# Attention with the keys on the partitions, 512 queries at a time, in rounded parts, in a two-block network kernel

## The reference, cut to what matters

```python
def one_block(qblk):
    s = jnp.einsum('bqhgd,bkhd->bhgqk', qblk, k, preferred_element_type=jnp.float32) * scale
    p = jax.nn.softmax(s, axis=-1).astype(v.dtype)
    return jnp.einsum('bhgqk,bkhd->bqhgd', p, v)
...
y = jnp.concatenate([ya * jax.nn.silu(a_gate), yb * jax.nn.silu(b_gate)], axis=-1)
return y @ w_out
```

## Time and profile before

| | us |
|---|---|
| median of 3 runs | 4312.03 |
| lowest, highest | 4309.52, 4312.44 |
| the profiled execution | 4309.44 |
| its span in the profile | 4307.4 |
| attention: pooling products to the last unit | 360.0 to 670.5 |
| ev_out: first to last weight product | 672.0 to 821.2 |
| granted clock of TensorE, mean | 0.98 |

### The profile page before, as it was taken

One profiled execution on the slowest core, in us unless ns is written; L12 is line 12 of the kernel. 1 busy time (PEld: TensorE's weight loads), 2 busy tenths in 40 slices (PEclk: granted clock), 3 DMA queues, 4 the chain that ended last, 5 costly groups with the idle time before them and its releaser, 6 DMA issues.

```text
span 4307.4 us, 51362 instructions
## 1 busy us (share of the span) xinstructions
PE 4077.1 (95%) x20059; PEld 3120.8 (72%) x20059; DVE 2023.9 (47%) x2420; ACT 1270.5 (29%) x1883; POOL 1333.3 (31%) x791
## 2 busy tenths in 40 slices
PE   7999998899999998889999999999999899999998
PEld 5776775457777774578888788876766678878886
DVE  4263662864676776571443233324444654323322
ACT  3122330212222221231332232224554633223222
POOL 0530000011111111022344444434444544444443
PEclk8999999999999999999999999999999999999999
DMA  6111004331121115651233333321000033333333
GB/s 229 39 39 59 0 0 141 142 136 65 68 76 68 68 53 191 155 163 49 83 93 97 98 97 97 98 89 69 25 25 25 16 113 94 96 99 97 97 98 107
DMA packets 118829, 372.05 MB, mean 86 GB/s; under 512 B 18004, under 2 KB 33679, under 8 KB 114896
## 3 DMA queue, kind: packets, MB, share of 16 engines
q1 hardware_dynamic: 98960, 296.38, 22.1%
q0 software_dynamic: 12784, 59.50, 3.8%
q10 hardware_dynamic: 6928, 13.96, 0.9%
HBM read 329.37 MB, written 38.06 MB: 85 GB/s over the span
## 4 chain that ended last, share of the span: by engine, by line
PE 63%; issue 16%; DVE 8%; POOL 6%; DMA 3%; ACT 2%; SPq 0%; POOLq 0%; ACTq 0%; DVEq 0%
PE banks L276 22%; PE banks L3104 6%; POOL w_parts L261 6%; PE banks L1230 5%; PE banks L291 5%; PE banks L696 5%; PE banks L1605 4%; PE banks L982 3%; PE banks L3178 2%; PE banks L3207 2%; DVE neg_max L1061 2%; DMA w_ring<-in_weights 1%; PE banks L3194 1%; PE banks L1586 1%; PE banks L1636 1%
## 5 line engine op out<-in xcount | busy, mean ns | idle before, releaser
L261 POOL TENSOR_TENSOR w_parts<-w_ring,w_parts 128x1024 fp32r<-128x1024 f32 x344 | 843.1, 2452 | 1089.3 <-ACT w_parts L254 1087.2
L276 PE MATMUL banks<-x_high,w_parts 128*128 128x512 f32 x2944 | 912.1, 390 | 0.0
L254 ACT ACTIVATE w_parts<-w_ring 128x1024 fp32r<-128x1024 f32 x344 | 364.5, 1060 | 1281.7 <-PE banks L276 1273.8
L276 PEld LDWEIGHTS banks<-x_high,w_parts 128*128 128x128 f32 x2944 | 552.6, 188 | 116.8 <-issue 2.1
L276 PE MATMUL banks<-x_low,w_parts 128*128 128x512 f32 x1472 | 572.8, 389 | 0.0
L276 PE MATMUL banks<-hidden_high,w_parts 128*128 128x512 f32 x1600 | 482.2, 392 | 6.0 <-POOL w_parts L261 6.0
L3312 DVE TENSOR_TENSOR_SCAN arena<-arena,flags 128x128 f32<-128x128 f32 (+3 forms) x192 | 248.7, 1308 | 250.3 <-ACT arena L3253 248.5
L276 PEld LDWEIGHTS banks<-hidden_high,w_parts 128*128 128x128 f32 x1600 | 301.7, 189 | 71.0 <-POOL w_parts L261 6.8
L2993 DVE TENSOR_TENSOR hidden_high<-banks,gate_temps 128x512 f32 (+1 forms) x88 | 60.9, 692 | 571.7 <-PE banks L276 571.6
L276 PEld LDWEIGHTS banks<-x_low,w_parts 128*128 128x128 f32 x1472 | 276.3, 188 | 59.0 <-issue 1.9
L1230 PE MATMUL banks<-parts_b,w_ring_low 128*128 128x512 f32 x896 | 303.6, 405 | 14.7 <-DVE resid_low L394 9.7
(11 more groups left out here) (456 smaller groups left out, 6488.4 us busy)
## 6 DMA issues: line engine op xcount, KB each, us to landing
w_ring<-in_weights SPq DMA_DIRECT2D x488, 512.0 KB, 3.5
arena<-in_hy_dft SPq DMA_DIRECT2D x11, 1536.0 KB, 6.1
s_cl<-arena POOLq DMA_DIRECT2D x4, 1152.0 KB, 6.7
resid<-in_xT ACTq DMA_DIRECT2D x2, 2048.0 KB, 26.3
resid<-in_xT POOLq DMA_DIRECT2D x1, 4096.0 KB, 14.0
arena<-in_fn_seq POOLq DMA_DIRECT2D x1, 4096.0 KB, 18.0
resid_spill<-resid POOLq DMA_DIRECT2D x1, 4096.0 KB, 12.6
s_e<-arena POOLq DMA_DIRECT2D x4, 1024.0 KB, 5.1
```

Of the source, the lines that this page charges most:

```text
L254: nc.scalar.activation(WP[:, g % 2, 0, :], WR[:, (g % RING) * TILE:(g % RING + 1) * TILE], ACT.Identity).then_inc(w_hi, 1)
L261: nc.gpsimd.tensor_tensor(WP[:, g % 2, 1, :], WR[:, (g % RING) * TILE:(g % RING + 1) * TILE], WP[:, g % 2, 0, :].bitcast(F32), ALU.subtrac ...
L276: mm = nc.tensor.matmul(PS[:, bank + h // H, :], w[a][:, k % KB, :], srcs[b][:, k, at + h:at + h + H], start=(first and i + q == 0), stop= ...
```

## The change

One half is now 512 queries of one head (12 halves), and a block is 128 of the 1280 keys (120 blocks in all, index i; half g, block b in it). Keys are on the partitions, queries on the free axis, so nothing is transposed.

- Keys, queries and values are split in rounded parts: high by ScalarE (`keys_high`, `queries_high`, `values_high`), low by GpSimd (`keys_low`, `queries_low`, `values_low`), all in memory that `resid` and `arena` leave free.
- The maximum of a query is still needed. `tops` multiplies 128 queries by 1280 keys, high parts only, into banks 4 to 6; VectorE's `top` takes the maximum. Four of these are turned by one transpose (`turned`), VectorE's `shift` spreads them on four partitions, and a fourth product of each block, of four rows, subtracts them (`MINUS`, `SHIFT`).
- `scores`: three products of parts and that fourth one, into bank i % 4. ScalarE takes the exponential twice, once unrounded (`PROB`), once rounded (`PPARTS[0]`). GpSimd's `prob_low` is their difference. `values`: three products of parts into bank 7.
- VectorE's `summed` adds `PROB` over the ten blocks; `denominator` sums it over the partitions by a product with ones; `divided` takes the reciprocal of 512 columns and multiplies; `gated` multiplies by the gate before.
- Three buffers each for `PROB` and its parts: the exponential of block i waits for sum and low part of block i-3 and, for the rounded copy, for its value products.
- The load of x is issued when the last value products are done, in two halves, as the parts of keys and values lie there. TensorE begins ev_out's modulation tiles one VectorE step earlier.
- Loops are written out.

```diff
...
-    A_P, A_PT, A_QC = A_S0, A_S0 + 2 * KEYS, A_S0 + 4 * KEYS
...
+    SHIFT = [PTB_[:, 8192 + 3584:8192 + 4096], s0_parts(7040, H)]
+    PROB = [ar(A_S0 + 4 * H + i * H, H) for i in range(3)]
+    PPARTS = [[s0_parts(7 * H + i * H, H) for i in range(3)], [s0_parts(at_, H) for at_ in (5120, 5632, 6400)]]
+    VPARTS = [[t[:, at_ + kv * KEYS:at_ + (kv + 1) * KEYS].rearrange("p (b n) -> p b n", b=KEYS // P)
+               for kv in range(N_KV)] for t, at_ in ((PTB_, 8192), (XLOW_, 2 * N_KV * KEYS))]
+    ACCP = [ar(2560 + i * H, H) for i in range(2)]
+    MINUS = s0_parts(6912, P)
+    TOP = [ar(A_S0 + 7552 + 4 * i, 4) for i in range(2)]
...
+    KBL = KEYS // P
+    HALVES = 2 * N_HEADS
+    BLOCKS = KBL * HALVES
...
+            def tops(g, t):
+                p.wait_ge(a_hi, parts_made(g))
+                p.wait_ge(a_top, 4 * g + t)
+                if t == 0 and g >= 3:
+                    p.wait_ge(a_o, 2 * (g - 2))
                 for c in range(0, KEYS, H):
                     w = min(H, KEYS - c)
...
+                    mm = nc.tensor.matmul(PS[:, 4 + c // H, 0:w], QPARTS[g % 2][0][:, t * P:(t + 1) * P],
+                                          KPARTS[0][kv_of(g)][:, c:c + w], start=True, stop=True)
+                mm.then_inc(a_mx, 1)
+            def turned(g):
+                p.wait_ge(a_top, 4 * g + 4)
+                if g:
+                    p.wait_ge(a_sh, g)
+                nc.tensor.transpose(PS[0:4, 6, 384:512], TOP[g % 2], IDENT[:, :]).then_inc(a_tt, 1)
+            def scores(i):
+                g, b = divmod(i, KBL)
+                kv, q = kv_of(g), QPARTS[g % 2]
+                if b == 0:
+                    p.wait_ge(a_lo, parts_made(g))
+                if i == 2:
+                    p.wait_ge(pme, 4)
+                if i >= 4:
+                    p.wait_ge(a_p, i - 3)
+                out_ = PS[:, i % 4, :]
+                for n, (x, y) in enumerate(((0, 0), (0, 1), (1, 0))):
+                    nc.tensor.matmul(out_, KPARTS[x][kv][:, b * P:(b + 1) * P], q[y], start=(n == 0), stop=False)
+                if b == 0:
+                    p.wait_ge(a_sh, g + 1)
+                nc.tensor.matmul(out_, MINUS[0:4, :], SHIFT[g % 2][0:4, :], start=False, stop=True).then_inc(a_s, 1)
+            def values(i):
+                g, b = divmod(i, KBL)
+                p.wait_ge(a_pl, i + 1)
+                if b == 0:
+                    p.wait_ge(a_lo, 3 if g < HALVES // N_KV else 6)
+                    if g:
+                        p.wait_ge(a_o, 2 * g - 1)
+                for n, (x, y) in enumerate(((0, 0), (1, 0), (0, 1))):
+                    mm = nc.tensor.matmul(PS[:, 7, :], VPARTS[x][kv_of(g)][:, b, :], PPARTS[y][i % 3],
+                                          start=(b + n == 0), stop=(b == KBL - 1 and n == 2))
+                mm.then_inc(a_pv, 1)
+            def denominator(g):
+                p.wait_ge(a_ad, KBL * (g + 1))
+                p.wait_ge(a_top, 4 * min(g + 3, HALVES))
+                nc.tensor.matmul(PS[:, 4, :], ONES[:, :], ACCP[g % 2], start=True, stop=True).then_inc(a_dn, 1)
+            pool_part(0, 0)
+            pool_part(0, 1)
+            tops(0, 0)
+            pool_part(1, 0)
+            tops(0, 1)
+            pool_part(1, 1)
+            tops(0, 2)
+            tops(0, 3)
+            turned(0)
+            scores(0)
+            scores(1)
+            for n in range(BLOCKS // 2):
+                g, s = divmod(n, KBL // 2)
+                ahead = g + 1 < HALVES
+                for i in (2 * n + 2, 2 * n + 3):
+                    if i < BLOCKS:
+                        scores(i)
+                if s < 2 and ahead:
+                    tops(g + 1, 2 * s)
+                if s == 2 and ahead:
+                    turned(g + 1)
+                if s == 3 and g:
+                    denominator(g - 1)
+                values(2 * n)
+                values(2 * n + 1)
+                if s < 2 and ahead:
+                    tops(g + 1, 2 * s + 1)
+            denominator(HALVES - 1)
...
+            nc.scalar.activation(MINUS, ONES[:, :], ACT.Identity, scale=-1.0)
+            keys_high(0)
+            queries_high(0)
+            a.wait_ge(pme, 4)
+            values_high(0)
+            for i in range(BLOCKS):
+                a.wait_ge(a_s, i + 1)
+                if i >= 3:
+                    a.wait_ge(a_pl, i - 2)
+                    a.wait_ge(a_ad, i - 2)
+                nc.scalar.activation(PROB[i % 3], PS[:, i % 4, :], ACT.Exp, scale=SCALE0)
+                if i >= 3:
+                    a.wait_ge(a_pv, i - 2)
+                nc.scalar.activation(PPARTS[0][i % 3], PS[:, i % 4, :], ACT.Exp, scale=SCALE0).then_inc(a_p, 1)
+                if i % KBL == 0 and i // KBL + 1 < HALVES:
+                    queries_high(i // KBL + 1)
+                if i == 0:
+                    keys_high(1)
+                    values_high(1)
...
-            g.dma_start(XT, ins["xT"].rearrange("(k p) t -> p k t", p=P)).then_inc(x_back, 16)
...
+            def top(g, t):
+                v.wait_ge(a_mx, 4 * g + t + 1)
+                nc.vector.reduce_max(TOP[g % 2][:, t:t + 1],
+                                     PS[:, 4:7, :].rearrange("p b t -> p (b t)")[:, 0:KEYS], AX_X).then_inc(a_top, 1)
+            def shift(g):
+                v.wait_ge(a_tt, g + 1)
+                nc.vector.tensor_tensor(SHIFT[g % 2][0:4, :].rearrange("q (t n) -> q t n", t=4),
+                                        PS[0:4, 6, 384:512].unsqueeze(1).broadcast_to([4, 4, P]),
+                                        IDENT[0:4, 0:4].unsqueeze(2).broadcast_to([4, 4, P]),
+                                        ALU.mult).then_inc(a_sh, 1)
+            def summed(i):
+                g, b = divmod(i, KBL)
+                acc = ACCP[g % 2]
+                v.wait_ge(a_p, i + 1)
+                if b == 1:
+                    if g >= 2:
+                        v.wait_ge(a_dn, g - 1)
+                    nc.vector.tensor_tensor(acc, PROB[(i - 1) % 3], PROB[i % 3], ALU.add).then_inc(a_ad, 2)
+                elif b > 1:
+                    v.wait_ge(a_ad, i)
+                    nc.vector.tensor_tensor(acc, acc, PROB[i % 3], ALU.add).then_inc(a_ad, 1)
...
+            def gated(g):
+                v.wait_ge(a_pv, KBL * (g + 1))
+                nc.vector.tensor_tensor(mixed_part(g), PS[:, 7, :], BG[:, g * H:(g + 1) * H], ALU.mult).then_inc(a_o, 1)
+            def divided(g):
+                v.wait_ge(a_dn, g + 1)
+                link(nc.vector.reciprocal(PS[:, 4, :], PS[:, 4, :]))
+                v.wait_ge(a_o, 2 * g + 1)
+                nc.vector.tensor_tensor(mixed_part(g), PS[:, 4, :], mixed_part(g), ALU.mult).then_inc(a_o, 1)
...
+            for n in range(BLOCKS // 2):
+                g, s = divmod(n, KBL // 2)
+                ahead = g + 1 < HALVES
+                if s == 0 and g:
+                    gated(g - 1)
+                summed(2 * n)
+                summed(2 * n + 1)
+                if s < 2 and ahead:
+                    top(g + 1, 2 * s)
+                    top(g + 1, 2 * s + 1)
+                if s == 2 and ahead:
+                    shift(g + 1)
+                if s == 3 and g:
+                    divided(g - 1)
+            gated(HALVES - 1)
+            divided(HALVES - 1)
...
+            def prob_low(i):
+                g_.wait_ge(a_p, i + 1)
+                if i >= 3:
+                    g_.wait_ge(a_pv, i - 2)
+                nc.gpsimd.tensor_tensor(PPARTS[1][i % 3], PROB[i % 3], PPARTS[0][i % 3].bitcast(F32),
+                                        ALU.subtract).then_inc(a_pl, 1)
...
+            keys_low(0, 1)
+            queries_low(0)
+            values_low(0, 3)
+            for i in range(BLOCKS):
+                prob_low(i)
+                if i == 3:
+                    queries_low(1)
+                if i == 5:
+                    keys_low(1, 5)
+                if i == 8:
+                    values_low(1, 6)
+                if i % KBL == 3 and i > KBL and i // KBL + 1 < HALVES:
+                    queries_low(i // KBL + 1)
+            g_.wait_ge(a_pv, BLOCKS)
+            for k in (0, 4):
+                g_.dma_start(XT[:, k:k + 4, :], xt[:, k:k + 4, :]).then_inc(x_back, 16)
...
             st = EvOut.st
-            wait_done(p, Attention.done)
+            p.wait_ge(a_o, 2 * HALVES - 1)
             for n in range(8):
                 if n:
                     p.wait_ge(mrow_out, 6 + n)
                 for i in range(3):
                     mod_rows(p, st, 4 * n + i, 7, i * P)
+                if n == 0:
+                    wait_done(p, Attention.done)
...
             wait_done(v, Attention.done)
-            v.wait_ge(x_back, 16)
+            v.wait_ge(x_back, 32)
```

More of the change, by code:

```diff
@@ L935, in _build @@
         after = EvIn.done
-        done = [(a_o, UNITS), (pme, 4)]
-        def cycles(eng, fn, link=None, per=0):
-            def run(lo, hi, loop):
-                if not loop:
```

(38 more changed lines are left out.)

175 lines of the change are left out of this document (35 added, 140 removed).

## The result

The kernel after takes 4320.22 us (median of 10 runs, 4315.49 to 4325.68), the kernel before beside it 4312.23 (10 runs): ratio 1.0022, 95% interval 1.0013 to 1.0031 (the two medians alone give 1.0019). It is slower by a little, 8 us, where 4309 was forecast. The profiled execution took 4317.33 (span 4315.5), 7.9 above that of before.

What follows compares the result with a forecast made beforehand. TensorE's arithmetic bounds the kernel now; afterwards VectorE with port waits would, at 24.0 us a half. Stage -3.4, clock after the tail +1.0, reload +1.0: -1.4, so 4309 us from 4312.0; range 4270 to 4336.

Steps and rivals of the forecast that it cites:

- The failed step: TensorE's scores, each block: the four-row product subtracting the maximum takes 0.233 us, bounds 0.12 and 0.43.
- 19.6: TensorE's work for a half in us: blocks 16.3, maxima 2.3, denominator 0.86, turn 0.1; four old units take 24.8.
- VectorE's walk: Attention's steady half, queues walked in order: VectorE with waits for the SBUF port shared with GpSimd needs 24.0 us.
- the blocks named: VectorE's sums of blocks 1, 3, 5, 6 and 7, held by GpSimd's low parts; five of nine over 1.0 us.
- Rivals 1: VectorE's sums in rounds 1 and 2 take the port first: 22.0 us a half, 4287; chance 0.20.
- 2: VectorE's sums and GpSimd's subtractions hardly meet on the port: 19.8 us a half, 4263; chance 0.08.
- 4: Every VectorE sum waits out a full GpSimd subtraction: +6.2 us a half, 4378; chance 0.03.
- 3: GpSimd keeps the port for its next queued subtraction, delaying block 1's sum: +1.27 us a half, 4324; chance 0.11.
- The start's clock: Attention's start: thinly used TensorE runs at the low 1.2 GHz; 2.2 us added, bounds 0 and 3.5.
- The tail: Last half, without maxima: +21.4 us from its round 1 to the output projection, which starts at 668.7.
- The reload: Loading x at the stage's end delays fn_seq and a weight tile in the projection: 1.0 us, bounds 0 and 7.
- Rival 5: Clock falls inside the stage as TensorE idles twice a half: +1.2 us a half, 4323; chance 0.08.

Runs made afterwards that it cites:

- e1_rows128: Kernel after with the product that subtracts the maximum on 128 rows (124 zeros) in place of four: 4307.1 us, ratio 0.9992 to before.
- e3: Kernel after with GpSimd's low parts of the exponentials cut to 8 of 512 columns, four-row product kept: 4316.3 us, ratio 1.0011 to before.
- e6: Kernel after with the product that subtracts the maximum on 64 rows (4 to 63 zero) in place of four: 4318.3 us, ratio 1.0019 to before.
- e10_paired: Kernel after with a round's two four-row products side by side behind both blocks' scores: 4301.2 us, ratio 0.9980 to before.

## Why the prediction was wrong

- **The failed step: "The product with four rows of weights has no row: its bounds are 0.12 (half of 0.233) and 0.43; I take 0.233, as its columns do."** It took 0.43, the upper bound, and the product behind it 0.2 more, which was in no bound. No row stands behind the 0.43 in the prediction, so that it was met to the hundredth is no merit of it. Ten of each a half are 10 x 0.2 + 10 x 0.2 = 4.0 us: 19.6 + 4.0 = 23.6, and two waits of 0.29 for the maxima 24.2, against 24.38 measured. I had named this ("Wrong would be: a 4-row product or a 512 exponential off its row by over 0.1 us, since each recurs 120 times") and yet gave it no rival. By its upper bound alone TensorE's sum would have been 21.6, under VectorE's 24.0; it was the cost to the neighbour that made TensorE the bound. Of the 11.4 us by which the stage missed its forecast, this step is 5.9: 3.4 in the halves and 2.45 in the tail. The other 5.5 are the start.
- **VectorE's walk was right, but for a TensorE that waits for it.** With the product's price removed, e1_rows128 shows half 23.78 (walk 24.0), tail 29.03 (29.45), five held sums in the blocks named, TensorE waiting for the maxima, clock 1.00; its time is 4307.1 (forecast 4309). In the kernel after itself four sums are held, in part other ones. Rivals 1, 2 and 4 (half 22.0, 19.8, all sums held) didn't occur; nor did 3.
- **The start's clock** I had at 2.2, bounds 0 to 3.5. The first exponential came where forecast (14.95 us after the stage's first product, 15.4 in the walk). After it 5.5 was lost beyond the 2.2, in two stretches at the low clock, of which I had only the first; 4.2 to 5.4 of it are absent in e1, e3 and e6. What sets that clock stays open.
- **The tail:** +2.45, of which e1_rows128 has none: the four-row product again.
- **The reload:** fn_seq takes 24.6 to land for 18.0, and lands 8.0 later against the projection (27.0 us behind its first product, 19.0 before), where I had some 5; the 1.0 taken for it is neither refuted nor confirmed.
- **Rival 5** didn't occur: in the steady half of the kernel after TensorE idles 0.3 us at a time, and the clock is 1.00.
- **The direction** turned on this: the stage came out 8.05 longer than before where 3.4 shorter was forecast (it starts 2.15 earlier and the projection 5.90 later). Less the 5.9 it would still have been 2.2 longer, so the start's 5.5 was needed for it too. The measured 4320 lies in the range, which was wide enough to hold the forecast, rivals 1, 3 and 5 and this.

## What to carry to other kernels

Put together a stream of products with the same number of weight rows; where one of few rows must stand among those of 128, pad it with zeros or gather several side by side, and price a lone one at 0.4 us, 0.2 for itself and 0.2 for the product behind it. Keep a running sum that VectorE adds to while GpSimd works in a PSUM bank: one operand from there is enough. Where two engines' sums for a period come out within a microsecond of each other, measure the term that has no row before trusting either, with what it costs its neighbours: its upper bound alone (21.6) would still have left VectorE's sum on top. Undoing one bound alone showed 4 or 13 us here, both together 49.

## What the runs showed of the hardware that I had not expected

- A product of 512 columns whose weight rows differ from its neighbours' takes 0.43 us in place of 0.233, alike with 4, 32 and 64 rows, and the next one 0.2 more; two of the same count in a row pay once (0.66). The load itself isn't longer (0.18 for 4 rows, 0.53 for three of 128); it isn't issued ahead of the product. The Trainium skill (TensorE: Matmul & The Clock Gate, LDWEIGHTS (loading the stationary operand)) says that a load's time doesn't depend on its rows. With that the trace agrees; the cost here lies in when the load starts.
- The granted clock came back later in starts with products of 4 or 32 rows (0.50 against 0.88 to 1.00 in the same 8 us; e10_paired had its 0.50 one stretch later), in one profile of each kernel. e1_rows128 and e6_rows64 have starts 4.2 and 4.5 us shorter than the kernel after; that the rows are the cause isn't shown.
- A sum with one operand in PSUM isn't touched by GpSimd's work (0.69 on average over 68), one with both in SBUF takes up to 1.74 (e1_rows128).
